# A two-layer decoder trunk on one core: the down projection of the MLP by Strassen's scheme, with weight sums on GpSimd and the residual kept by tokens

## What is computed

```
for l in range(2):
    u = rms_norm(x, norm1_w[l])
    proj = u @ w_in[l]                       # 1024 -> 6928 columns: branches and gates
    branch g = P_g(conv | gated linear attention | windowed attention)
    mixed = sum_g sigmoid(gate_g) * (branch_g @ w_branch[l, g])
    x = x + mixed @ w_o[l]                   # 1024 x 1024
    h = rms_norm(x, norm2_w[l])
    x = x + square(relu(h @ w_up[l])) @ w_down[l]   # 1024 -> 4096 -> 1024
```

## Time and profile before

| | before |
|---|---|
| median of 3 runs | 1655.81 us |
| the profiled execution, its own time | 1654.38 us |
| its span (first to last instruction) | 1652.6 us |
| TensorE busy | 1617.4 us (98%) |
| VectorE busy | 926.8 us (56%) |
| ScalarE busy | 628.0 us (38%) |
| GpSimd busy | 0.2 us |
| DMA | 150.92 MB, mean 91 GB/s |

### The profile page before, as it was taken

How to read it: one execution, slowest core, us unless ns; L and a number is a source line. 1 busy time by engine, 2 the same in 40 slices (tenths; PEclk the granted TensorE clock), 3 DMA queues, 4 the chain that set the end, 5 groups by cost and what they waited for, 6 DMA issues and landing times.

```text
span 1652.6 us, 22309 instructions
## 1 busy us (share of the span) xinstructions
PE 1617.4 (98%) x7656; PEld 1326.4 (80%) x7656; DVE 926.8 (56%) x1365; ACT 628.0 (38%) x1000; POOL 0.2 (0%) x4
## 2 busy tenths in 40 slices
PE   5999999999999999999999999999999999999997
PEld 4877778888888888888887777888888888888886
DVE  5576675455565444454656667654456544445456
ACT  5446652233343142323435566432234322323242
POOL 0000000000000000000000000000000000000000
PEclk9999999999999999999999999999999999999999
DMA  4331123233333223332322212133223332333221
GB/s 145 103 102 52 52 82 98 77 102 102 102 102 100 92 89 102 102 102 80 102 82 99 77 52 78 52 108 122 77 76 128 101 99 82 102 102 102 85 93 51
DMA packets 135659, 150.92 MB, mean 91 GB/s; under 512 B 4848, under 2 KB 122128, under 8 KB 135568
## 3 DMA queue, kind: packets, MB, share of 16 engines
q1 hardware_dynamic: 135136, 149.69, 28.3%
q10 hardware_dynamic: 432, 0.08, 0.0%
HBM read 147.67 MB, written 2.10 MB: 91 GB/s over the span
## 4 chain that ended last, share of the span: by engine, by line
PE 95%; DVE 2%; ACT 1%; DVEq 1%; DMA 0%; issue 0%; ACTq 0%; SPq 0%
PE acc L454 27%; PE acc L455 27%; PE acc L456 27%; PE acc L485 3%; PE acc L487 3%; PE acc L486 3%; PE bank L639 1%; PE bank L658 1%; PE bank L650 1%; PE bank L597 1%; PE bank L611 0%; DMA x_tokens<-in_x_dram 0%; DVE x_tokens L1342 0%; PE bank L570 0%; PE bank L586 0%
## 5 line engine op out<-in xcount | busy, mean ns | idle before, releaser
L454 PE MATMUL acc<-uh,wh 128*128 128x512 f32 x1152 | 454.8, 395 | 8.8 <-DVE wl L951 7.6
L456 PE MATMUL acc<-uh,wl 128*128 128x512 f32 x1152 | 449.9, 391 | 0.0
L455 PE MATMUL acc<-ul,wh 128*128 128x512 f32 x1152 | 449.9, 391 | 0.0
L742 ACT ACTIVATE wh<-raw 128x1024 fp32r<-128x1024 f32 x227 | 238.8, 1053 | 280.9 <-PE acc L456 269.0
L454 PE MATMUL acc<-yh,wh 128*128 128x512 f32 (+1 forms) x832 | 324.4, 390 | 0.6 <-DVE yl L1263 0.6
L455 PE MATMUL acc<-yl,wh 128*128 128x512 f32 (+1 forms) x832 | 324.2, 390 | 0.0
L456 PE MATMUL acc<-yh,wl 128*128 128x512 f32 (+1 forms) x832 | 324.2, 390 | 0.0
L951 DVE TENSOR_TENSOR wl<-raw,wh 128x1024 fp32r<-128x1024 f32 x227 | 278.0, 1225 | 48.5 <-ACT wh L742 30.5
L454 PEld LDWEIGHTS acc<-uh,wh 128*128 128x128 f32 x1152 | 216.8, 188 | 59.8 <-issue 14.5
L456 PEld LDWEIGHTS acc<-uh,wl 128*128 128x128 f32 x1152 | 216.7, 188 | 45.7
L455 PEld LDWEIGHTS acc<-ul,wh 128*128 128x128 f32 x1152 | 217.0, 188 | 43.5
(11 more groups left out here) (182 smaller groups left out, 1237.2 us busy)
## 6 DMA issues: line engine op xcount, KB each, us to landing
raw<-in_w_in_dram SPq DMA_DIRECT2D x40, 1024.0 KB, 5.2
raw<-in_w_up_dram SPq DMA_DIRECT2D x32, 1024.0 KB, 5.3
raw<-in_w_down_dram SPq DMA_DIRECT2D x32, 1024.0 KB, 5.0
raw_branch<-in_w_in_dram SPq DMA_DIRECT2D x12, 1024.0 KB, 4.9
raw_branch<-in_w_branch_dram SPq DMA_DIRECT2D x12, 1024.0 KB, 5.0
raw<-in_w_o_dram SPq DMA_DIRECT2D x8, 1024.0 KB, 5.0
x_tokens<-in_x_dram SPq DMA_DIRECT2D x4, 512.0 KB, 5.5
raw_kv<-in_w_in_dram SPq DMA_DIRECT2D x4, 512.0 KB, 3.8
```

Of the source, the lines that this page charges most:

```text
L454: nc.tensor.matmul(acc[b][:], h[:, k, :], right_h(k), start=k == 0, stop=False)
L455: nc.tensor.matmul(acc[b][:], h[:, k, :], right_l(k), start=False, stop=False)
L456: return nc.tensor.matmul(acc[b][:], lo[:, k, :], right_h(k), start=False, stop=k == n - 1)
L742: nc.scalar.activation(split_view(True, base, pos), raw_view(base, pos), ACT.Copy).then_inc(hi_done, 1)
```

## The change

**Strassen's scheme for the down projection** (the form with 7 products and 15 sums). In each quarter the hidden block [512 tokens x 1024] and the weight block [1024 x 1024] are cut into 2 x 2 blocks, A11 to A22 (256 tokens x 512 features) and B11 to B22 (512 x 512). Instead of 8 block products there are 7, `p0` to `p6`, of the left sides A11, A12, S2, S1, A11-A21, S4, A22 and the right sides B11, B21, B12'+B11, B22-B11', B12' = B22-B12, B22, B21-B11'. A product is 2 units ("dn", one for each `pair` of contraction tiles), each with 2 token tiles x 2 contraction tiles x 3 passes = 12 matmuls (`product`, L527 to L529): 168 matmuls of 512 columns in a quarter, where there were 192. Hidden features stand still and weights move, so results have tokens on partitions.

**Sums of hidden blocks** (hs_sum, hd_sum) are made by VectorE from `hidden`; they are split into high and low like the rest. Relu and square are now both on ScalarE. **Sums of weight blocks** are made by GpSimd in the loaded buffers themselves (8 operations of 128x1024 a quarter, L976 to L986); each waits until VectorE has made the low half of the block that it overwrites, and `split_high` of p2 and p3 waits for `weights_summed`. Weights of the down side have buffers of their own (`raw_down`, 2 x 2 MB), so the raw slots serve the rest.

**Results:** p1, p5 and p6 go straight into x, scaled per token. p0, p2, p3, p4 are summed over the quarters in `product_sums` and combined into x in the last quarter of a layer only.

**The residual** stays as x_tok [128, 4, 1024], tokens on partitions. W_o becomes a token unit ("wa", "wb"). For each norm TensorE transposes x (`transposed_x`, L543, words UT0 to UT7 and V0 to V7, 4 transposes each), ScalarE and VectorE read uh and ul from PSUM, and the sum of squares is one ScalarE activation per token tile (`square_sum`). The sums over partitions and the transposes at the very end are gone; the output leaves in 8 pieces of 256 KB. All Fori loops are unrolled, and the three order lists are new.

Core of the diff:

```diff
-                        unit(l, M0, q, pos, u_tile(yh), u_tile(yl), hid_ready, ...)   # 8 down units
+            def product(l, q, i, pair):
+                u, key = f"dn{14 * q + 2 * i + pair}", f"p{7 * q + i}"
+                n = l * QUARTERS + q
+                h, lo = wh_rows[UNIT[u] % SPLIT], wl_rows[UNIT[u] % SPLIT]
+                pe.wait_ge(lo_done, unit_at(l, u) + 1)
+                ready, first = ((hid_ready, 8 * n), (hid_ready, 8 * n + 4), (sums_ready, 4 * n), (sums_ready, 4 * n),
+                                (diff_ready, 4 * n), (sums_ready, 4 * n), (hid_ready, 8 * n + 4))[i]
+                pe.wait_ge(ready, first + 2 * pair + 2)
...
+        @block.gpsimd
+                    for pair in range(PAIRS):
+                        pool.wait_ge(down_full[pair], (l * QUARTERS + q + 1) * 32)
+                        G.tensor_tensor(b12[pair], b22[pair], b12[pair], ALU.subtract)
+                    for pair in range(PAIRS):
+                        G.drain()
+                        low_half_done(l, q, 0, pair)
+                        G.tensor_tensor(b11[pair], b12[pair], b11[pair], ALU.add).then_inc(weights_summed, 1)
+                    for pair in range(PAIRS):
+                        G.drain()
+                        low_half_done(l, q, 2, pair)
+                        G.tensor_tensor(b21[pair], b21[pair], b11[pair], ALU.subtract)
+                        G.drain()
+                        G.tensor_tensor(b11[pair], b22[pair], b11[pair], ALU.subtract).then_inc(weights_summed, 1)
...
+            def split_high(l, u):
+                if u.startswith("dn"):
+                    n, i = step_of(u)[1] // 14 + l * QUARTERS, step_of(u)[1] % 14 // 2
+                    if i == 0:
+                        act.wait_ge(down_full[UNIT[u] % 2], (n + 1) * 32)
+                    elif i in (2, 3):
+                        act.wait_ge(weights_summed, 4 * n + 2 * (i - 2) + UNIT[u] % 2 + 1)
...
+                        V.tensor_tensor(s1, hid[:, k, 2 * P:], hid[:, i, 2 * P:], ALU.add)
+                        V.tensor_tensor(s2, s1, hid[:, k, 0:2 * P], ALU.subtract)
+                        V.tensor_tensor(s4, hid[:, i, 0:2 * P], s2, ALU.subtract).then_inc(sums_val, 1)
...
+                            if q == 0:
+                                V.tensor_copy(g, a[:]).then_inc(free, 1)
+                            else:
+                                V.tensor_tensor(g, g, a[:], ALU.add).then_inc(free, 1)
+                        if not final:
+                            continue
+                        if i == 0:
+                            scaled_into_x(t, 0, g1)
+                            V.tensor_tensor(g6, g6, g1, ALU.add)
...
+            def transposed_x(l, name, ready, count):
+                b = open_bank(l, name)
+                pe.wait_ge(ready, count)
+                k = step_of(name)[1]
+                for t in range(TT):
+                    last = nc.tensor.transpose(b[:, t * P:(t + 1) * P], x_tok[:, t, k * P:(k + 1) * P], ident)
+                last.then_inc(bank_full, 1)
```

More of the change, by code:

```diff
@@ new lines, with add_fills @@
+ACC_USE, ACC_USES = {}, [0] * 4
+for _key, _banks in ACC_BANKS.items():
+    for _b in _banks:
+        ACC_USES[_b] += 1
+        ACC_USE[_key, _b] = ACC_USES[_b]
+TILE_OF = {}
+for _key, _banks in ACC_BANKS.items():
+    if len(_banks) > 1:
+        TILE_OF[_key] = sum(len(ACC_BANKS[k]) - 1 for k in TILE_OF)
+TILES = sum(len(ACC_BANKS[k]) - 1 for k in TILE_OF)
+FILL = {}
+def add_fills(layer, words):
+    for word in words:
+        FILL[layer, word] = len(FILL)
+add_fills(0, [f"UT{k}" for k in range(KT // 2, KT)])
@@ new lines, in _, with residual @@
+                                split_ahead(l, f"br{i}")
+                mixed_low(KT - 1)
+                for pair in range(PAIRS):
+                    V.drain().then_inc(down_free[pair], 1)
+                def residual(key, t, half):
+                    a, free = tile_ready(dve, l, key, t)
+                    x_at = x_tok[:, t, half * SEQ:(half + 1) * SEQ]
+                    V.tensor_tensor(x_at, a[:], x_at, ALU.add).then_inc(free, 1)
+                    V.drain().then_inc(x_upd, 1)
```

1037 lines of the change are left out of this document (543 added, 494 removed).

## The result

The changed kernel takes **1692.95 us** (median of 4 runs, 1692.54 to 1693.03) where the kernel before takes 1656.30 on the same chip (4 runs, 1655.64 to 1656.96): ratio 1.022, 95% interval 1.020 to 1.024. It is slower by 37 us; the forecast was 1634.5, with a range up to 1690. The profiled execution is one of 1692.95 us, with a span of 1691.2.

The account below looks back on a forecast made before the run. TensorE was taken as the bound, busy 98%. 1654.4 - 43.5 + 12.6 - 4.5 - 9.1 - 3.8 + 6 + 21 = 1633.1 for the profiled execution, median 1.4 higher: 1634.5 us; range 1612 to 1690.

Parts of the forecast that it names:

- 0.4 a quarter: Step from up to down side: VectorE without a gap lets dn3 start at T+8.5, due at T+8.2; 0.4 us a quarter.
- 0.8 a quarter: Down side: dn7 waits for GpSimd's four weight sums and the split behind them, 0.8 us a quarter at 2.0 us each.
- GpSimd and VectorE shut each other out: Rival: VectorE instructions with two SBUF inputs and GpSimd operations wait for each other; about 6 a quarter, 1682 us, chance 0.34.
- g = 2.0: Time of one GpSimd operation of 128x1024, taken as the middle between bounds of 1.23 and 2.83 us.
- nothing up to g = 1.8, above that 4g - 7.2 a quarter: Wait of dn7 on GpSimd's sums, with g the time of one GpSimd operation: start T+12.2+4g, due T+19.4.
- If TensorE falls to the lower clock in those gaps, more is lost than the gaps themselves: Closing remark on TensorE's gaps: a lower clock there would cost more than the gaps; no size given.
- So VectorE bounds it: 5.8: Last quarter of each layer: VectorE's 16 more combining steps make dn13's split late, T+41.2 against T+35.4; 5.8 us.
- +6: Where layers meet: TensorE idles for sums in x, ul and square sums; +6 us, between 0 and 10.
- -43.5: Down products on TensorE: 192 fewer matmuls over 8 quarters at 0.227 us each; -43.5 us.
- +12.6: Transposes on TensorE: 28 groups of four now in the stream, 0.45 us a group; +12.6 us.
- -9.1: End of the kernel: 4.3 us after the last matmul instead of 13.4; -9.1 us.
- -3.8: Start of the kernel: first matmul near 19.4 instead of 23.5; -3.8 us, between +3 and -8.

Follow-up runs that it names:

- The exclusion without any chain: Changed kernel with GpSimd's eight sums replaced by the same operations on a spare tile nobody reads, p2 and p3 split without waiting: 1658.46 us.
- Two fills: Changed kernel with each of GpSimd's eight sums replaced by two write-only fills of the same tile, all waits and signals kept: 1635.05 us.
- three fills: Changed kernel with each of GpSimd's eight sums replaced by three write-only fills of the same tile, all waits and signals kept: 1673.13 us.
- leaving the 16 steps out: Changed kernel without weight sums, and also without the 16 steps combining product sums into x in each layer's last quarter: 1606.98 us.
- the run without sums: Changed kernel without all eight sums of weight blocks a quarter and the waits for them, GpSimd doing nothing in the MLP: 1623.80 us.
- the new list for VectorE: Changed kernel with weight sums made by VectorE instead of GpSimd and VectorE's MLP order rewritten for four kinds of quarter: 1635.36 us.
- handing over two of the eight sums: Kernel with weight sums on VectorE and its order rewritten, but the two sums B22-B12 a quarter given back to GpSimd: 1636.40 us.
- the second version on VectorE: Against a first kernel with weight sums on VectorE (1658.13 us): two hidden-sum low halves, and one first-quarter weight sum, moved behind dn4's split: 1669.28 us.

## Why the prediction was wrong

- **The step that failed: "0.4 a quarter" at dn3 and "0.8 a quarter" for GpSimd are worked out as if the two engines didn't touch each other.** The sum takes VectorE's rows at the durations that they have beside an idle GpSimd and says of GpSimd's first four operations "the up side to hide in, if they disturb nobody": the exclusion stands in the sum at nothing. The runs show in its place dn3 late by 3.2 us (4.4 to 4.5 in a layer's first quarter), dn6 and dn7 by 2.6 together, a wait of 3.5 more in each last quarter, and about 1.7 of clock where it falls: the second quarter's products take 45.85 us where the forecast had 39.3. The exclusion without any chain costs 34.7 us.
- **"GpSimd and VectorE shut each other out", chance 0.34.** This rival is what happened, and it was weighed too low. The reason given against it was that no row before showed the two engines together. But nothing in those rows spoke against it either, and the new order put the pair side by side in every quarter. Its mechanism was told right: dn3 late by about 3.3 (measured 3.2), GpSimd's two B11 sums at about T-11 and T-5 (T-10.8 and T-3.8), results read from PSUM untouched, the chain to dn7 stretched by VectorE's splits. Of its signs, the longer rows of 128x256 and over 3 us at dn3 were found, but not over 3 us at dn7: it waits 0.8, and dn6, which the text left out, 1.8. Its price, 6 a quarter on top of the forecast's 1.2, makes 7.2, and measured are 7.7. That is partly luck: the waits are 5.8, and the other 1.9, nearly all of it the lower clock, was not in the price. Its own range, 1660 to 1695, held the result; the range given for the whole, up to 1690, left its end out and missed by 3 us.
- **"g = 2.0".** Measured 2.40 where GpSimd is not held up, so the formula gives 2.4 a quarter instead of 0.8, 13 us in all; this alone would still have left the change the faster at 1647. The bounds of 1.23 and 2.83 held for that; held up by VectorE, an operation lasts up to 3.2. The middle was too low. The Trainium skill's figure (GPSIMD Engine Reference, Performance versus the Vector engine) gave an estimate of 2.25, nearer than the middle, and 6% under the row.
- **"nothing up to g = 1.8, above that 4g - 7.2 a quarter".** Two fills (g = 1.95) gave 1.1 of waits a quarter where the formula has 0.6; three (2.95) gave 5.4 where it has 4.6. Only dn7 was counted; dn6 is on the chain too, behind two operations, a split and p1's result: 2.7 late with three fills.
- **"If TensorE falls to the lower clock in those gaps, more is lost than the gaps themselves".** Said, but with no price in the sum or in the rivals. Of the 81 us that the products are too long, 54 are waits by the list, and about 15 of the other 27 are some 70 matmuls 0.43 apart instead of 0.227; the rest lies in starts a little further apart around the waits and wasn't followed up.
- **"0.4 a quarter" at dn3.** Without GpSimd nothing is left there: 38.2 us a quarter. The count was 0.4 too high.
- **"So VectorE bounds it: 5.8"** in the last quarter. Right in kind: dn5, dn9, dn11 and dn13 wait 0.7 to 1.4 each there, as the text had it, and leaving the 16 steps out takes 16.8 us from two layers. 4.6 of it is the wait where layers meet, a part of the "+6" (there the changed kernel has 8.1 us from dn12's last matmul to dn13's first, of which 1.8 are transposes and 0.2 a matmul: 6.0). What the text didn't have is the wait of 3.5 in the middle of dn4, which only the exclusion brings.
- **"-43.5", "+12.6", "-9.1" and "-3.8"** stand. The products' matmuls are 0.227 apart (168 in 38.2 us where nothing waits). The start and the end of the changed kernel, against the earlier trace rows, and a place where 16 transposes stand in the stream:

```profile
20.14 0.77 PE L478 MATMUL acc<-uh,wh 128*128 128x512 f32 x1 [7.05 <-DVEq L1025]
...
35.52 0.48 PE L478 MATMUL acc<-uh,wh 128*128 128x512 f32 x1
...
486.95 0.39 PE L480 MATMUL acc<-uh,wl 128*128 128x512 f32 x1
487.19 1.91 PE L543 MATMUL bank<-consts,x_tokens 128*128 128x128 f32 x16
...
489.16 0.40 PE L479 MATMUL acc<-ul,wh 128*128 128x512 f32 x1
...
1687.40 0.39 PE L529 MATMUL acc<-wl_rows,hidden_hi 128*128 128x512 f32 x1
1687.83 0.75 DVE L1390 SCALAR_TENSOR_TENSOR x_tokens<-acc,rsqrt_tokens_mlp_sq,x_tokens 128x512 f32<-128x512 f32 x1 [0.23 <-PE acc L529]
```

The first matmul stands at 20.1 (forecast 19.4) and the one behind the spread at 35.5 (35.5). From 486.95 to 489.16 are 2.21, less the usual 0.45: 1.76 for four groups, 0.44 each (0.45). The span ends 3.4 us after the last matmul's end (4.3). That these terms were sound is seen in the run without sums: the forecast without GpSimd's 0.8 a quarter is 1626.7 for the profiled execution, and that run's is 1622.96, most of the difference being the 0.4 at dn3 (3.2 in all) that isn't there.

So one pair of engines made the whole miss. The forecast gave 0.36 to a slower kernel. What was open before the run, whether the pair would collide, could not be read from the profile of a kernel in which GpSimd was idle; it could be weighed, and was weighed too low.

Not tried: the change with its eight sums on GpSimd under the new list for VectorE, and Strassen's scheme without the residual by tokens or the other way round, so the two halves of the change are told apart by the trace and the sum alone.

## What to carry to other kernels

An idle GpSimd is not free help for a VectorE that has no gap: each operation of GpSimd that reads SBUF holds up a VectorE operation with both inputs in SBUF until it is over (2.67 us for 0.42 here), so its price is read from VectorE's gaps at that place, not from its own queue. When a change puts work next to an engine's busiest stretch, ask first who is late there and by how much, then count what each wait also costs in clock. And before work is given to another engine, rewrite the order of the one that has it, with the PSUM banks in the count: here that was worth 23 us, and handing over two of the eight sums nothing.

## What was not expected of the hardware

- After the wait of 3.02 us at dn3 the granted clock was 0.50 for 3.4 us, and 8 matmuls were done in place of 15: 1.7 us on top of the wait. In the run with the exclusion alone dn3's 2.2 us or more were followed in every quarter by 7 or 8 matmuls about 0.43 apart, begun up to 1.9 us after dn3. But no such stretch followed dn4's 2.4 us in the middle quarters of the second version on VectorE, nor dn3's 3.2 us in the last quarters of the changed kernel itself (granted clock 1.00 from 807.6 to 811.0), so the length of one wait doesn't settle it. In the middle quarters that took 38.2 to 39.6 us (no sums, two fills, new list) the clock did not fall.
- GpSimd's addition of 128x1024 lasts 2.40 us on different tiles and 1.89 when both inputs are one tile; a copy lasts 1.04, a fill 0.96.
- GpSimd is held up by VectorE as well as the other way round: its 2.40 us become 3.19 when a split of VectorE stands before it.
